# Two-stream joins of the triangular solve, with unread full-size products between them and the two transposes ahead swapped

## The reference, cut to what matters

```python
kb = kc * bc[..., None]
a_mat = jnp.where(strict, jnp.einsum('nbhid,nbhjd->nbhij', kb, kc) * decay, 0.0)
eye = jnp.eye(CHUNK, dtype=f32)
t_inv = lax.linalg.triangular_solve(eye + a_mat, jnp.broadcast_to(eye, a_mat.shape),
                                    left_side=True, lower=True, unit_diagonal=True)
u_val = jnp.einsum('nbhij,nbhjd->nbhid', t_inv, vb)
w_key = jnp.einsum('nbhij,nbhjd->nbhid', t_inv, kb * jnp.exp(gc)[..., None])
```

## Time and profile before

| what | value |
|---|---|
| time, median of 3 runs | 1657.66 us (1656.71 to 1664.1) |
| span of the profiled execution | 1656.5 us |
| TensorE busy | 1362.0 us (82%) |
| VectorE, ScalarE, GpSimd busy | 573.7, 432.4, 218.2 us |
| read from HBM | 525.94 MB, 318 GB/s over the span |
| the joins, from the end of the first transpose to the start of the scan | 191.4 to 218.5 us |
| mean granted TensorE clock over the span | 0.896 |

### The profile page before, as it was taken

How to read it: one execution, slowest core, us unless ns; L and a number is a source line. 1 busy time by engine, 2 the same in 40 slices (tenths; PEclk the granted TensorE clock), 3 DMA queues, 4 the chain that set the end, 5 groups by cost and what they waited for, 6 DMA issues and landing times.

```text
span 1656.5 us, 21997 instructions
## 1 busy us (share of the span) xinstructions
PE 1362.0 (82%) x9592; PEld 901.7 (54%) x9592; DVE 573.7 (35%) x1131; ACT 432.4 (26%) x647; POOL 218.2 (13%) x119
## 2 busy tenths in 40 slices
PE   6999999999999997667577577999977757665678
PEld 2798697999999972222122122998732212221227
DVE  2676724888347620110010011687201101101106
ACT  3445335544454220000000001675210000000005
POOL 0307322588420000000000000000000000000000
PEclk9999889999999998887878788999987878878889
DMA  9314425444555989999999999559899999999992
GB/s 402 136 50 170 211 96 223 151 165 147 177 201 190 394 360 428 426 426 429 428 426 426 428 425 413 204 181 358 330 426 426 429 427 427 426 427 427 428 410 105
DMA packets 52482, 528.45 MB, mean 319 GB/s; under 512 B 4768, under 2 KB 4896, under 8 KB 20128
## 3 DMA queue, kind: packets, MB, share of 16 engines
q1 hardware_dynamic: 51808, 525.22, 77.5%
q10 hardware_dynamic: 576, 1.79, 0.3%
HBM read 525.94 MB, written 1.05 MB: 318 GB/s over the span
## 4 chain that ended last, share of the span: by engine, by line
PE 55%; DMA 37%; DVE 5%; ACT 2%; issue 1%; SPq 1%; POOL 0%; DVEq 0%; ACTq 0%; POOLq 0%
PE bank L648 25%; DMA ring<-in_w_gate 11%; PE bank L1212 9%; DMA work<-in_w_down 8%; DMA ring<-in_w_up 7%; DMA work<-in_w_up 6%; PE bank L1232 5%; DMA ring<-in_w_down 4%; PE bank L1294 3%; PE bank L1362 2%; PE bank L641 1%; PE bank L720 1%; PE bank L1091 1%; PE bank L832 1%; DMA ring<-in_dense 1%
## 5 line engine op out<-in xcount | busy, mean ns | idle before, releaser
L1212 PE MATMUL bank<-ring,work 128*32 128x512 f32 x1232 | 319.7, 735 | 138.1 <-DMA ring<-in_w_up 71.6
L648 PE MATMUL bank<-work_rounded,ring_rounded 128*128 128x256 f32 (+1 forms) x2032 | 313.1, 289 | 2.2 <-DVE work_rounded L1992 1.3
L648 PEld LDWEIGHTS bank<-work_rounded,ring_rounded 128*128 128x128 f32 x2032 | 274.0, 189 | 10.8 <-issue 2.9
L648 PE MATMUL bank<-xn_rounded,ring_rounded 128*128 128x256 f32 (+1 forms) x1472 | 248.3, 284 | 1.1 <-DVE xn_rounded L2026 1.1
L1212 PEld LDWEIGHTS bank<-ring,work 128*32 128x32 f32 x1232 | 69.8, 130 | 303.7 <-issue 109.2
L648 PEld LDWEIGHTS bank<-xn_rounded,ring_rounded 128*128 128x128 f32 x1472 | 202.6, 188 | 5.5 <-issue 2.6
L2525 DVE TENSOR_TENSOR work<-work,bank 128x512 f32<-128x512 f32 x16 | 11.0, 688 | 540.8 <-PE bank L1212 540.8
L1892 POOL TENSOR_TENSOR ring_rounded<-ring,ring_rounded 128x2048 fp32r<-128x2048 f32 (+1 forms) x37 | 158.0, 4289 | 195.6 <-ACT ring_rounded L1435 195.6
L1212 PE MATMUL bank<-work 128*32 128x512 f32 x496 | 154.0, 666 | 33.9 <-DMA work<-in_w_gate 19.1
L1435 ACT ACTIVATE ring_rounded<-ring 128x2048 fp32r<-128x2048 f32 (+1 forms) x78 | 136.6, 1797 | 58.2 <-PE bank L648 34.1
L1960 POOL TENSOR_TENSOR work<-work_rounded,work 128x128 f32<-128x128 f32 x32 | 12.1, 399 | 1059.5 <-PE bank L1269 727.7
(11 more groups left out here) (328 smaller groups left out, 1765.7 us busy)
## 6 DMA issues: line engine op xcount, KB each, us to landing
ring<-in_dense SPq DMA_DIRECT2D x48, 2048.0 KB, 8.4
ring<-in_w_up SPq DMA_DIRECT2D x38, 2048.0 KB, 30.0
ring<-in_w_gate SPq DMA_DIRECT2D x36, 2048.0 KB, 30.0
ring<-in_w_down SPq DMA_DIRECT2D x34, 2048.0 KB, 29.3
work<-in_w_gate SPq DMA_DIRECT2D x16, 2048.0 KB, 22.7
work<-in_w_down SPq DMA_DIRECT2D x16, 2048.0 KB, 33.1
spare<-in_w_gate SPq DMA_DIRECT2D x8, 2048.0 KB, 29.0
work<-in_w_up SPq DMA_DIRECT2D x8, 2048.0 KB, 33.0
```

Source lines behind the costliest of these rows:

```text
L648: last = mm(out, rv(high_store[r][:, at:at + P]), rv(x[part][k]), start=opens and k == 0 and j == 0, stop=closes and k == n_k - 1 and j == 2)
L1212: ins = mm(out[slots(y), :], xg[:, k, slots(y)], expert_columns(w, at, 512), start=k == 0, stop=k == KT - 1)
```

## The change

Four things change, all in the joins.

1. The joins of 32 run over both pairs product by product instead of pair after pair; `p6x` runs over both directions product by product. `p6` keeps its order. Semaphores are raised at the same products as before, but since the pairs now end together, the half ends for both at once. `p5x` waits for both copies of a half before its first product of it, `p6x` likewise.
2. DVE writes `half_v` first, then `half_u`. TensorE starts `p5` after the first of the two (`solved` at 1), and `p5x` after the second; ACT's copies of the diagonal blocks, which read `half_v` alone, wait for the first too. POOL waits for both as before.
3. A new helper `awake(b)` multiplies the constant matrix of ones (128 x 128) with 256 columns of the constants, into a bank whose content is not needed. Nobody reads the product. There are 11 of them: two ahead of `p5`, while nothing else is ready, one within `p5`, two within `p5x`, four ahead of the groups of `p6`, and two ahead of the halves of `p6x`.
4. Nothing else: the arithmetic that is read, its operands and its banks are the same.

```diff
-        pe.wait_ge(S["solved"], 2)
+        def awake(b):
+            mm(bank[b][:, 0:SEQ], ones, consts[:, 0:SEQ], start=True, stop=True)
         pe.wait_ge(S["att_ready"], 4)
+        awake(7)
+        awake(7)
+        pe.wait_ge(S["solved"], 1)
...
         for s in range(2):
-            for pair in range(2):
-                first, second = slice(64 * pair, 64 * pair + 32), slice(64 * pair + 32, 64 * pair + 64)
-                for i, (d, u, h) in enumerate(of_half(s)):
+            for i, (d, u, h) in enumerate(of_half(s)):
+                for pair in range(2):
+                    first, second = quarters(pair)
                     last = mm(bank[4 + 2 * s + pair][second, 32 * i:32 * i + 32], amat[first, d, u, h, second],
                               half_v[first, d, u, h], start=True, stop=True)
-                signal(last, "p5_mm")
+                    if i == 15:
+                        signal(last, "p5_mm")
+                if i == 7 and s == 0:
+                    awake(7)
+        pe.wait_ge(S["solved"], 2)
...
             for pair in range(2):
                 pe.wait_ge(S[("p5_act", "p5_dve")[pair]], s + 1)
-                for i, (d, u, h) in enumerate(of_half(s)):
+            for i, (d, u, h) in enumerate(of_half(s)):
+                for pair in range(2):
...
+                if i == 7:
+                    awake((3, 7)[s])
...
             for d in range(2):
+                awake(((7, 7), (0, 0))[s][d])
                 for i, (_, u, h) in enumerate(of_half(s, d)):
...
             for d in range(2):
                 pe.wait_ge(S[("p6_act", "p6_dve")[d]], s + 1)
-                for i, (_, u, h) in enumerate(of_half(s, d)):
+            awake((3, 5)[s])
+            for i, (_, u, h) in enumerate(of_half(s, 0)):
+                for d in range(2):
...
-        act.wait_ge(S["solved"], 2)
+        act.wait_ge(S["solved"], 1)
...
+        signal(v.transpose(half_v.rearrange("p d u h c -> p c (d u h)"), inverse.rearrange("p r c -> p c r")), "solved")
         signal(v.transpose(half_u.rearrange("p d u h c -> p c (d u h)"), inverse), "solved")
-        signal(v.transpose(half_v.rearrange("p d u h c -> p c (d u h)"), inverse.rearrange("p r c -> p c r")), "solved")
```

More of the change, by code:

```diff
@@ L912, in of_half, with quarters @@
             return [(i, u, h) for i in ((0, 1) if d is None else (d,)) for u in (2 * s, 2 * s + 1) for h in range(HEADS)]
-        pe.wait_ge(S["solved"], 2)
+        def quarters(pair):
+            return slice(64 * pair, 64 * pair + 32), slice(64 * pair + 32, 64 * pair + 64)
+        def awake(b):
+            mm(bank[b][:, 0:SEQ], ones, consts[:, 0:SEQ], start=True, stop=True)
         pe.wait_ge(S["att_ready"], 4)
+        awake(7)
+        awake(7)
+        pe.wait_ge(S["solved"], 1)
         for b in range(2):
@@ L937, in _ @@
                         last = mm(out[second], half_u[second, d, u, h], p5[second, d, u, h], start=True, stop=True)
-                signal(last, "p5x_mm")
+                    if i == 15:
+                        signal(last, "p5x_mm")
+                if i == 7:
+                    awake((3, 7)[s])
         first, second = slice(0, 64), slice(64, 128)
@@ L961, in _ @@
                         last = mm(out[second], side[second, u, h], p6[second, d, u, h], start=True, stop=True)
-                signal(last, "p6x_mm")
+                    if i == 7:
+                        signal(last, "p6x_mm")
         def key_weights(n):
```

## The result

The changed kernel takes 1666.22 us (median of 12 runs, 1662.45 to 1668.64), the kernel before beside it 1658.99 us (12 runs, 1656.71 to 1664.1). The ratio is 1.0037, with a 95% interval of 1.0023 to 1.0051: some 7 us slower by the medians (6 by the ratio), where +2.2 was forecast, and 1.2 us above the upper end of the range. The profiled execution has a span of 1666.2 us and a time of its own of 1667.94 us, the second slowest of the twelve; the profiled execution of the kernel before (1656.71 us) was the fastest of its twelve. So a difference between the two traces overstates the usual one.

What follows compares the result with a forecast made beforehand. The prediction took the joins as bound by TensorE at half clock, much of the time using one part of the array. Front -1.6, p5x -0.5, p6 with p6x +4.3 gave +2.2 us: 1659.9 us, range 1649.5 to 1665.

Steps and rivals of the forecast that it cites:

- Whether the clock stays up: Joins: the granted clock was expected to fall at 194 to 198 us and stay at half until the scan.
- the row at 846 us: Trace from 846.2 to 849.5 us, read as full-size work in 1.27 of 3.3 us before the clock fell to 0.50.
- The first rival: Joins: the clock stays at 1.00 and TensorE ends at 211.8 us; -7 us, 1650.6 us; chance 0.16.
- Front and `p5x`: Start of the joins: p5x starts at 197.1 us, -1.6 us, and takes 5.9 instead of 6.4 us, -0.5 us.
- the prediction's sum without products: Joins without the unread products' cost: -1.6 - 2.6 - 2.0 = -6.2 us.
- The -1.6 us: Front: with the transposes swapped, p5x starts at 197.1 us, after ACT's first copy, instead of 198.73.
- The price of an unread product: Joins: each costs 1.05 us at half clock, 0.83 plus 0.22 for two shape steps; bounds 0.83 and 1.4.
- The clock's return: Start of the scan: the moment the clock comes back got no term, only 1.5 us either way in the bounds.
- I pass [it] on to the end in full: After the joins: a shift arising at 200 us moves all later work and reaches the kernel's end whole.

Runs made afterwards that it cites:

- e10_wait_filled: The changed kernel plus four full-size unread products in TensorE's wait between p5 and p5x; 1652.3 us against 1659.13, ratio 0.9956.
- e12_wait_small: The changed kernel plus 28 unread products of 32 x 32 in TensorE's wait between p5 and p5x; 1664.46 us against 1658.7, ratio 1.0033.
- e1_no_products: The changed kernel without its eleven unread products, new order and swapped transposes kept; 1653.32 us against 1658.42, ratio 0.9972.
- e7_order_only: The kernel before with only the new order of products, no swap and no unread products; 1652.04 us against 1658.03, ratio 0.9969.
- e3_swap_only: The kernel before with only the two transposes swapped and their waits adapted; 1658.08 us against 1658.42, ratio 1.0004.
- e5_again: The changed kernel, unchanged, run again in a second batch; 1664.38 us against 1658.03, ratio 1.005.
- e8_routing: The changed kernel plus five unread products around the second block's routing; 1668.47 us against 1658.03, ratio 1.0076.
- e11_only_wait: e1_no_products plus four unread products in TensorE's wait between p5 and p5x; 1653.81 us against 1659.13, ratio 0.9971.

## Why the prediction was wrong

**Whether the clock stays up: right, with one of its two reasons not borne out.** The clock fell at 196.8 us, inside the 194 to 198 us of the forecast, and stayed at 0.50. Of the reasons given, that nothing of full size runs between the product in `p5` and the first in `p5x` is the one that e10_wait_filled and e12_wait_small bear out. The other, that nine products in 20 us are too few, was judged by the row at 846 us, and that row was misread: 1.06 of its 1.27 busy us are products of line 1232 with a stationary operand of 128 x 32, which is a quarter of the array and not full-size work.

```profile
846.41 1.06 PE L1232 MATMUL bank<-ring,work 128*32 128x512 f32 x6
```

With four more products in the wait, the same eight on the path kept the clock at 1.00 for the 15 us to the scan; no run holds it with the nine alone. The forecast also saw a wait of at most a microsecond: it priced `p5` at half clock, to end at 196.8 us. It ran at full clock and ended at 195.18, which left the 1.78 us in which the clock fell.
The first rival (the clock stays at 1.00, -7 us) describes e10_wait_filled, which has the scan 6.2 us earlier and -6.8 us. Its sum came out by two errors that offset each other: `p5x` took 3.6 us and not 5.1, since its rows come 0.010 us apart at full clock, and a product cost 0.77 us and not 0.65.
The Trainium skill (TensorE: Matmul & The Clock Gate, HAM oscillation — how this bites in real kernels) puts the fall down to idle gaps between matmuls. e10_wait_filled, with no gap and no fall, goes with it. e12_wait_small goes against it: no gap up to the fall, and the clock at 0.50 from 198.9 us. In the changed kernel the clock did fall in a gap, but in one of 1.78 us, shorter than the waits that the section describes.

**Front and `p5x`: the sum right, in part by luck.** `p5x` was forecast to start at 197.1 us and last 5.9; it starts at 196.96 and lasts 6.15 us. But the 5.9 were 3.8 us of rows and 2.1 of products, and the 6.15 are 3.5 and 2.7: the rows were dearer in the forecast and the products cheaper. Alternation over three parts gives 0.018 us per row over whole halves, not only at a seam. With that over two parts in `p6x` it is worth 5 to 6 us by e1_no_products and e7_order_only, where the prediction's sum without products was -6.2. The -1.6 us were put down to the swap; e3_swap_only gets them from the swap alone, e7_order_only from the new order alone.
The Trainium skill (TensorE: Matmul & The Clock Gate, Wait — 56ns, not 53.3ns?) has starts never closer than about 25 ns. Here, between different parts of the array, they are 18 ns apart at half clock, and in e10_wait_filled three per 0.03 us, 10 ns apart, at full clock.

**The price of an unread product: the step that failed first.** Its term was "1.05 us at half clock", 0.83 for the product and 0.22 for two steps between shapes. It measured 1.34 us: 0.85 and 0.49. The one step of 0.11 us that could be read was between small shapes. In the changed kernel's timeline 1.15 us lie between the product at 203.11 us and the first row of `p6`, 0.30 more than its own 0.85; the 16 rows are through at 205.97 us, and the next product comes 0.19 us later. In `p5x` the cheaper rows hid it. From 203.11 us to the scan the six products of `p6` and `p6x` make 6 x 0.29 = 1.7 us more than forecast, and that is the difference of the scan's start: 222.39 us against the forecast's 220.7. The bounds held this (0.83 to 1.4); the value taken was too near the low end.

**The clock's return: no term, and it was +1.0 us.** The scan's third group of products starts at 228.47 us, 6.1 us after the first, since the clock comes back only at 227.5, 5.1 us after the start. Before, it was back 3.0 us after the start. This is inside the 1.5 us that the range gave it.

**"I pass [it] on to the end in full": held for 950 us and failed in the second block.** The shift of 4.9 us after the joins arrives at the first copy whole (5.0 us) and is 9.9 us at the second. The forecast looked for no change of the clock far from the joins. In e5_again the loss there is smaller, and e7_order_only has the same low mean of 0.89 without a product. From the forecast of 1659.9 to 1666.22 us are 6.3 us: 1.7 of price, 1.0 of the clock's return, 1.3 because the kernel before has its median at 1658.99 us over twelve runs and not at 1657.66, and the 2.3 left over fit the second block, where the profiled execution lost 4.9 and e5_again 1.7. The mean clock of whole executions speaks for it: 0.8928 over the twelve runs of the changed kernel, 0.8953 over the 83 runs of the kernel before that are on record beside the experiments; the 3 us that the joins are longer at 0.50 make 0.001 of this. And among those 83 runs the slower ones have the lower clock, about 1.1 us per 0.001. Still that split is argued and not shown: no run holds the second block's clock fixed. Whether the changed kernel meets the low stretch more often than the kernel before, and why, stays open. e8_routing showed only that five full-size products there don't help.

## What to carry to other kernels

Small products that follow each other should go to different parts of the array: here that alone gave 5 to 6 us of 27 in the joins and cost nothing. Unread work that is to hold TensorE's clock belongs above all where TensorE waits, where it cost next to nothing here, and here it had to be full-size; between small products each one cost 1.6 to 1.7 times its own rows, so that even where it worked, as in e10_wait_filled, it about paid for itself. And a wait that a change leaves behind (here 1.78 us for ScalarE's copy) is worth looking at in its own right: what ran in it decided the clock of the next 25 us.

## What the runs showed of the hardware beyond that

- Between small products a full-size one of 0.45 us at full clock costs 0.77 us, and one of 0.85 us at half clock costs 1.34 us; a second right behind it costs its 0.85 alone.
- 1.8 us of products of 32 x 32 in a row, with TensorE busy throughout, did as little to hold the clock as an empty wait. The moment of the fall says little: 198.9 us with the small products, and 196.8, 196.3 and 198.2 us in three executions of the same joins with the wait empty. In e1_no_products TensorE waited 3.39 us with the clock at 1.00, which fell at 198.5 us, 0.3 us into `p5x`.
- In the second half of `p5x` TensorE sometimes stops with nothing to wait for that the profile shows. In e7_order_only, e1_no_products and e11_only_wait:

```profile
200.64 0.21 PE L948 MATMUL bank<-ring 32*32 32x32 f32 x1 [0.91 <-issue]
```

```profile
202.50 0.20 PE L948 MATMUL bank<-ring 32*32 32x32 f32 x1 [1.46 <-issue]
```

```profile
199.43 0.18 PE L948 MATMUL bank<-ring 32*32 32x32 f32 x1 [1.24 <-issue]
```

  With full-size products in between, e8_routing has one of 0.30 us there, and e12_wait_small one of 0.41 us right behind `p5x`. Between 200.2 and 200.8 us, ahead of the gap in e1_no_products, the transfer view has one packet of instructions of 0.02 MB, and e7_order_only and e11_only_wait have such packets one to three microseconds ahead of theirs. But the changed kernel has such packets in `p5x` too, and no gap. Instructions that run out faster than they are loaded would look like this, but no run here tested it.
